# Three layer norms run tile by tile into the next product, and the last one stored in six parts

## What is computed

```
m = ada_modulation(c, w_ada, b_ada)
h = x * (1.0 + m[:, 1]) + m[:, 0]
x = post_norm_residual(x, swiglu(h, w_ffn1_in, w_ffn1_out), m[:, 2], 0.5, ln_g[0], ln_b[0])
h = x * (1.0 + m[:, 4]) + m[:, 3]
...
x = post_norm_residual(x, mix, m[:, 5], 1.0, ln_g[1], ln_b[1])
h = x * (1.0 + m[:, 7]) + m[:, 6]
x = post_norm_residual(x, swiglu(h, w_ffn2_in, w_ffn2_out), m[:, 8], 0.5, ln_g[2], ln_b[2])
```

## Time and profile before

| | |
|---|---|
| Median of 3 runs | 1078.45 us (1078.01 to 1084.59) |
| The profiled execution | 1081.01 us |
| Its span, first to last instruction | 1079.2 us |
| Mean granted clock of TensorE | 0.915 of full speed |
| TensorE matmul busy | 913.4 us, 85% of the span |
| VectorE, ScalarE, GpSimd busy | 543.2, 353.2, 36.5 us |

### The profile page before, as it was taken

One profiled execution on the slowest core, in us unless ns is written; L12 is line 12 of the kernel. 1 busy time (PEld: TensorE's weight loads), 2 busy tenths in 40 slices (PEclk: granted clock), 3 DMA queues, 4 the chain that ended last, 5 costly groups with the idle time before them and its releaser, 6 DMA issues. The chain is left out here.

```text
span 1079.2 us, 17658 instructions
## 1 busy us (share of the span) xinstructions
PE 913.4 (85%) x7201; PEld 814.6 (75%) x7201; DVE 543.2 (50%) x813; ACT 353.2 (33%) x505; POOL 36.5 (3%) x42
## 2 busy tenths in 40 slices
PE   3679999999998699988775599777739999999983
PEld 2369999998996699845654577556729999989982
DVE  0144444445655633386557544371664555555653
ACT  2122232223342333346425133340232332233322
POOL 0000000000000000010000000000500000000000
PEclk9679999999999799989899889876969999999996
DMA  9958889885556542747595783969402555434501
GB/s 271 310 158 235 242 246 257 244 236 136 160 169 209 185 145 76 237 163 231 158 384 167 270 278 103 372 217 290 134 22 79 156 154 144 130 99 134 160 1 49
DMA packets 232790, 199.95 MB, mean 185 GB/s; under 512 B 9489, under 2 KB 198045, under 8 KB 232582
## 3 DMA queue, kind: packets, MB, share of 16 engines
q1 hardware_dynamic: 229376, 190.87, 58.1%
q10 hardware_dynamic: 2278, 4.16, 1.3%
q0 software_dynamic: 1056, 3.80, 1.0%
HBM read 195.00 MB, written 3.80 MB: 184 GB/s over the span
## 5 line engine op out<-in xcount | busy, mean ns | idle before, releaser
L575 PE MATMUL B<-Hh,wh 128*128 128x320 f32 x960 | 291.1, 316 | 28.2 <-DVE Hl L1443 17.4
L576 PE MATMUL B<-Hl,wh 128*128 128x320 f32 x960 | 288.2, 313 | 0.0
L1406 DVE TENSOR_TENSOR wl<-raw,wh 128x2048 fp32r<-128x2048 f32 x90 | 208.1, 2313 | 147.2 <-ACT wh L1063 147.2
L1063 ACT ACTIVATE wh<-raw 128x2048 fp32r<-128x2048 f32 x90 | 172.3, 1914 | 161.9 <-PE B L580 111.6
L575 PEld LDWEIGHTS B<-Hh,wh 128*128 128x128 f32 x960 | 184.2, 192 | 38.4 <-issue 38.4
L576 PEld LDWEIGHTS B<-Hl,wh 128*128 128x128 f32 x960 | 184.3, 192 | 0.0
L580 PE MATMUL B<-Hh,wl 128*128 128x320 f32 x960 | 161.2, 310 | 0.0
L580 PEld LDWEIGHTS B<-Hh,wl 128*128 128x128 f32 x960 | 146.8, 189 | 0.0
L575 PE MATMUL B<-Gh,wh 128*128 128x320 f32 x352 | 104.0, 309 | 4.6 <-DVE Gl L1503 4.6
L576 PE MATMUL B<-Gl,wh 128*128 128x320 f32 x352 | 103.7, 309 | 0.0
L737 PE MATMUL B<-cst,ring 128*128 128x128 f32 x512 | 72.1, 301 | 30.0 <-DMA ring<-in_cache_k 11.8
(11 more groups left out here) (211 smaller groups left out, 835.8 us busy)
## 6 DMA issues: line engine op xcount, KB each, us to landing
raw<-in_w_ffn_in SPq DMA_DIRECT2D x88, 512.0 KB, 6.4
raw<-in_w_ada SPq DMA_DIRECT2D x72, 512.0 KB, 4.7
ring<-in_cache_k SPq DMA_DIRECT2D x128, 256.0 KB, 4.4
ring<-in_cache_v SPq DMA_DIRECT2D x128, 256.0 KB, 4.6
raw<-in_w_ffn_out SPq DMA_DIRECT2D x32, 384.0 KB, 3.6
raw<-in_w_mix_in SPq DMA_DIRECT2D x24, 512.0 KB, 4.8
raw<-in_w_ffn_out SPq DMA_DIRECT2D x32, 320.0 KB, 4.3
raw<-in_w_mix_out SPq DMA_DIRECT2D x4, 512.0 KB, 8.6
```

Source lines behind the costliest of these rows:

```text
L575: pe.matmul(out, w, xh[k], start=start and k == 0, stop=False)
L576: pe.matmul(out, w, xl[k], start=False, stop=False)
L1063: return act.activation(out, in_, func, **kw)
L1406: dve.tensor_tensor(wl[:, wbuf(n), :], raw_view(n), f32(wh[:, wbuf(n), :]), ALU.subtract).then_inc(lo_ready, 1)
```

## The change

- **Fused weights.** For the second and third sublayer `fuse_affine` folds g and b of the norm into the modulation's scale and shift, once, on vectors of 72 columns. The input of the next product is then made from `Z` directly, as `Z * rstd * scale + shift`, into a new buffer `scaled`; ScalarE adds the prompt's shift while it rounds.
- **Tile by tile.** `modulate` makes the samples first, then prompt tiles one at a time, two ahead of the `Hl` that VectorE makes between them. ScalarE rounds one tile at a time. `first_slot` replaces the first `pair_slot` of F1, MI and F2: its first bank takes tile k as soon as `Hh` and `Hl` of tile k are there, then comes the second bank, then the low weights of both.
- **Stream made later.** `X` of the first and second norm is made by `stream`, one tile behind each of eight `low` in MI, and behind each of eight slots of F2.
- **Mean and variance.** GpSimd adds six tiles; the last two go into the mean through matmuls of their own. Eps is the bias of ScalarE's root, which reads PSUM; L1477 goes.
- **Order.** In A2 two modulation slots come ahead of the mean and a third ahead of the variance, and ScalarE copies two rows before it squares. At the start `modulate(0)` comes ahead of `low(F1 + 1)`. In the second norm `low(F2 + 1)` moves behind the subtractions. ScalarE rounds the input of MI before it rounds the weights of MI + 1.
- **Output.** VectorE scales `X` per tile, ScalarE adds b, TensorE transposes in the order half, token tile; six PSUM banks are used, VectorE copies four groups and ScalarE two, and SyncE stores six parts. GpSimd's two stores and its last wait go.

```diff
+                fs = slice(512 * half, 512 * half + 512)
+                dst = o["y_prompt"][t0:t0 + tn, fs] if t < 2 else o["y_sample"][:, fs]
+                sp.dma_start(dst, xn[0:tn, t, fs]).then_inc(y_stored, 16)
...
+            def first_slot(t, kind, b0, s):
...
+                wait_high(t)
+                for h in range(2):
+                    for k in range(KT):
+                        if h == 0:
+                            pe.wait_ge(hh_ready, 9 * s + k + 2)
+                            pe.wait_ge(hl_ready, 9 * s + k + 2)
+                        pe.matmul(B[b0 + h][:, 0:N], part(vh, h, k), Hh[:, k, :], start=(k == 0), stop=False)
+                        pe.matmul(B[b0 + h][:, 0:N], part(vh, h, k), Hl[:, k, :], start=False, stop=False)
+                wait_low(t)
+                for h in range(2):
+                    for k in range(KT):
+                        m = pe.matmul(B[b0 + h][:, 0:N], part(vl, h, k), Hh[:, k, :], start=False, stop=(k == KT - 1))
+                m.then_inc(used, 1)
...
             def norm_mean(s):
                 pe.wait_ge(zsum_ready, s + 1)
-                pe.matmul(B[2][:, 0:N], C("mean"), zsum[:, :], start=True, stop=True).then_inc(mean_ready, 1)
+                pe.matmul(MEAN, C("mean"), zsum[:, :], start=True, stop=False)
+                pe.wait_ge(z_ready, KT * s + KT - 1)
+                pe.matmul(MEAN, C("mean"), Z[:, KT - 2, :], start=False, stop=False)
+                pe.wait_ge(z_ready, KT * s + KT)
+                pe.matmul(MEAN, C("mean"), Z[:, KT - 1, :], start=False, stop=True).then_inc(mean_ready, 1)
...
-                    pair_slot(At(F1 + 2 * j + 1, i, 4), "ffn_in", 2 * j)
+                    if i == 0 and j == 0:
+                        first_slot(At(F1 + 1), "ffn_in", 0, 0)
+                    else:
+                        pair_slot(At(F1 + 2 * j + 1, i, 4), "ffn_in", 2 * j)
...
+            first_slot(At(MI), "wide", 0, 1)
...
+            first_slot(At(F2), "ffn_in", 0, 2)
+            pair_slot(At(F2 + 1), "ffn_in", 2)
...
+            for n, (half, t) in enumerate(Y_GROUPS):
+                t0, tn = TILES[t]
+                for k in range(4 * half, 4 * half + 4):
+                    if t == 0:
+                        pe.wait_ge(x_final, k + 1)
+                    m = pe.transpose(Y_BANKS[n][0:tn, (k % 4) * P:(k % 4 + 1) * P], X[:, k, t0:t0 + tn], ident)
+                m.then_inc(y_T, 1)
...
             def round_input(s):
 
-                for j in range(4):
-                    act.wait_ge(h_ready, 4 * s + j + 1)
-                    act_(Hh[:, 2 * j:2 * j + 2, :], Z[:, 2 * j:2 * j + 2, :]).then_inc(hh_ready, 1)
+                src = scaled if s else Z
+                act.wait_ge(hs_ready, s + 1)
+                act_(Hh[:, :, S:N], src[:, :, S:N]).then_inc(hh_ready, 1)
+                for k in range(KT):
+                    act.wait_ge(h_ready, KT * s + k + 1)
+                    if s:
+                        act_(Hh[:, k, 0:S], src[:, k, 0:S], ACT.Identity, bias=mod[:, 3 * s * KT + k, 0:1]
+                             ).then_inc(hh_ready, 1)
+                    else:
+                        act_(Hh[:, k, 0:S], src[:, k, 0:S]).then_inc(hh_ready, 1)
...
             def norm_root(s):
-                act.wait_ge(veps_ready, s + 1)
-                act_(rstd[:, :], rstd[:, :], ACT.Sqrt).then_inc(std_ready, 1)
+                act.wait_ge(sq_used, 4 * s + 4)
+                act_(rstd[:, :], VAR, ACT.Sqrt, bias=C("eps")).then_inc(std_ready, 1)
...
-            norm_squares(0)
             for k in range(6):
                 if k == 2:
+                    norm_squares(0)
                     norm_root(0)
                 act.wait_ge(used, A2 + k + 1)
                 act.wait_ge(ada_comb, 29 + k)
                 act_(arow[:, k % 2, :], B[4 + k % 2][:, 0:256]).then_inc(ada_row, 1)
             high(At(MI))
+            round_input(1)
             high(At(MI + 1))
-            round_input(1)
...
+            for k in range(KT):
+                act.wait_ge(x_scaled, k + 1)
+                b = PRM_AT["ln_b"] + 2 * KT + k
+                act_(X[:, k, :], X[:, k, :], ACT.Identity, bias=prmT[:, b:b + 1]).then_inc(x_final, 1)
+            for n in Y_ON_ACT:
...
+            def fuse_affine(s):
+
+                sc, sh = mod[:, (3 * s + 1) * KT:(3 * s + 2) * KT, :], mod[:, 3 * s * KT:(3 * s + 1) * KT, :]
+                lo = (s - 1) * KT
+                g, b = [prmT[:, PRM_AT[name] + lo:PRM_AT[name] + lo + KT].unsqueeze(2).broadcast_to([P, KT, NC])
+                        for name in ("ln_g", "ln_b")]
+                step(dve.tensor_tensor(affine[:, :, :], sc, b, ALU.mult))
+                step(dve.tensor_tensor(sh, sh, affine[:, :, :], ALU.add))
+                step(dve.tensor_tensor(sc, sc, g, ALU.mult))
...
+                ds = dst[:, :, S:N].rearrange("p k (b t) -> p k b t", b=NB)
+                src = (Z if s else X)[:, :, S:N]
+                if s:
+                    r = rstd[:, S:N].unsqueeze(1).broadcast_to([P, KT, NS])
+                    step(dve.tensor_tensor(dst[:, :, S:N], src, r, ALU.mult))
+                    src = dst[:, :, S:N]
+                step(dve.tensor_tensor(ds, src.rearrange("p k (b t) -> p k b t", b=NB), samples(3 * s + 1), ALU.mult))
+                dve.tensor_tensor(ds, ds, samples(3 * s), ALU.add).then_inc(hs_ready, 1)
+
+                def prompt(k):
+                    sc = mod[:, (3 * s + 1) * KT + k, 0:1]
+                    if s:
+                        m = dve.scalar_tensor_tensor(out=dst[:, k, 0:S], in0=Z[:, k, 0:S], scalar=sc, in1=rstd[:, 0:S],
+                                                     op0=ALU.mult, op1=ALU.mult)
+                    else:
+                        m = dve.tensor_scalar(dst[:, k, 0:S], X[:, k, 0:S], sc, mod[:, k, 0:1], ALU.mult, ALU.add)
                     m.then_inc(h_ready, 1)
-                for j in range(4):
-                    dve.wait_ge(hh_ready, 4 * s + j + 1)
-                    dve.tensor_tensor(Hl[:, 2 * j:2 * j + 2, :], Z[:, 2 * j:2 * j + 2, :],
-                                      f32(Hh[:, 2 * j:2 * j + 2, :]), ALU.subtract).then_inc(hl_ready, 1)
+
+                def rest(k):
+                    dve.wait_ge(hh_ready, 9 * s + k + 2)
+                    hh = f32(Hh[:, k, 0:S])
+                    if s:
+                        m = dve.scalar_tensor_tensor(out=Hl[:, k, 0:S], in0=dst[:, k, 0:S],
+                                                     scalar=mod[:, 3 * s * KT + k, 0:1], in1=hh, op0=ALU.add,
+                                                     op1=ALU.subtract)
+                    else:
+                        m = dve.tensor_tensor(Hl[:, k, 0:S], dst[:, k, 0:S], hh, ALU.subtract)
+                    m.then_inc(hl_ready, 1)
+
+                prompt(0)
+                prompt(1)
+                dve.wait_ge(hs_ready, s + 1)
+                dve.wait_ge(hh_ready, 9 * s + 1)
+                dve.tensor_tensor(Hl[:, :, S:N], dst[:, :, S:N], f32(Hh[:, :, S:N]), ALU.subtract).then_inc(hl_ready, 1)
+                for k in range(KT):
+                    dve.wait_ge(h_ready, KT * s + k + 1)
+                    rest(k)
+                    if k + 2 < KT:
+                        prompt(k + 2)
...
+            def stream(s, k):
+
+                g, b = PRM_AT["ln_g"] + s * KT + k, PRM_AT["ln_b"] + s * KT + k
+                step(dve.scalar_tensor_tensor(out=X[:, k, :], in0=Z[:, k, :], scalar=prmT[:, g:g + 1], in1=rstd[:, :],
+                                              op0=ALU.mult, op1=ALU.mult))
+                step(dve.tensor_scalar(X[:, k, :], X[:, k, :], prmT[:, b:b + 1], None, ALU.add))
...
-                between(0)
-                dve.wait_ge(sq_used, 4 * s + 4)
-                dve.tensor_scalar(rstd[:, :], B[3][:, 0:N], LN_EPS, None, ALU.add).then_inc(veps_ready, 1)
...
+                between()
+                dve.wait_ge(d_ready, 4 * s + 4)
                 dve.wait_ge(std_ready, s + 1)
                 step(dve.reciprocal(rstd[:, :], rstd[:, :]))
-                for j in range(4):
-                    zj = Z[:, 2 * j:2 * j + 2, :]
-                    step(dve.tensor_tensor(zj, zj, two(rstd[:, :]), ALU.mult))
-                    for k in (2 * j, 2 * j + 1):
-                        g, b = PRM_AT["ln_g"] + s * KT + k, PRM_AT["ln_b"] + s * KT + k
-                        m = dve.tensor_scalar(X[:, k, :], Z[:, k, :], prmT[:, g:g + 1], prmT[:, b:b + 1],
-                                              ALU.mult, ALU.add)
-                    if s == 2 and j == 3:
...
             scale_vec(1)
             dve.wait_ge(x_copied, KT)
+            modulate(0)
             low(At(F1 + 1))
-            modulate(0)
             low(At(F1 + 3))
...
+            fuse_affine(1)
...
+            fuse_affine(2)
+
+            for k in range(8):
+                low(At(MI + k + 2))
+                stream(0, k)
...
+                if k < 3:
+                    low(At(MO + k + 2))
```

(11 more changed lines are left out.)

105 lines of the change are left out of this document (43 added, 62 removed).

## The result

| | before | changed |
|---|---|---|
| median of four runs each (us) | 1080.01 | 1046.41 |
| lowest to highest | 1078.01 to 1084.59 | 1037.77 to 1049.8 |
| ratio, 95% interval | | 0.967 [0.960, 0.974] |
| profiled execution, span (us) | 1081.01, 1079.2 | 1045.4, 1043.4 |
| mean granted clock | 0.915 | 0.923 |

The forecast was 1048.2, range 1038 to 1057. In a second comparison, five rounds on another chip, the changed kernel took 1042.26 and the one before 1081.97: 0.964 [0.959, 0.968]. An execution more than 1.5% above the fastest of its kernel counts as slow and is left out of the ratios; the only one here is the profiled one of `wait_all` (1058.22 us).

The account below looks back on a forecast made before the run. TensorE, busy 85% of the span, was taken to bound the kernel, with loss left at four stage edges: start and three norms. Gains 5.4 + 6.0 + 11.1 + 7.8 = 30.3 us off 1078.45 gave 1048.2 us, range 1038 to 1057.

Parts of the forecast that it names:

- The start, 5.4: Start to the end of F1's first slot: slot ends at 65.6 in place of 71.05, 5.4 us gained.
- the tile's 0.83 us: F1's first slot: VectorE makes one tile and the rest of another in 0.41 + 0.42 = 0.83 us.
- rival (1): First slots: the clock is already up when the second bank starts, 5.9 us less, 1042.3; chance 0.17.
- rival (4): F1 starts earlier than its weights can come, so the start's 5.4 us are lost, 1053.6; chance 0.05.
- The first norm, 6.0: First norm to the end of MI's first slot: it ends at 364.0 in place of 370.0, 6.0 us gained.
- The second norm, 11.1: Second norm to the end of F2's first slot: it ends at 806.5 in place of 817.7, 11.1 us gained.
- The last norm and output, 7.8: Third norm to the end: last copy at 1066.5 in place of 1073.58, and a faster store, 7.8 us gained.
- one add less and no L1477: Third norm: these two savings bring the reciprocal 1.6 us forward, to 1059.2.
- 0.7 for the store: After the last copy: a 256 KB part lands in 4.6 us where 5.6 stood, counted as 0.7 us gained.
- What I cost at nothing: Added `fuse_affine` and `stream` work on VectorE: covered by idle time; uncovered, all sixteen `stream` steps would cost 15 us.
- (2): First slots: the ScalarE-VectorE hand-over sets the pace, 1.2 us a tile, 8.6 us more, 1056.8; chance 0.10.
- (3): The clock doesn't come back in the first slots, 1054.2, chance 0.09; with many slots low, chance 0.02.

Follow-up runs that it names:

- wait_all: The changed kernel, but the first slots of F1, MI and F2 wait for all nine input parts: 1046.42 us, 0.968; repeated, 1052.18 us, 0.974.
- one_mean: The changed kernel, but GpSimd adds all eight tiles and the mean is one matmul: 1046.09 us, 0.970.
- two_stores: The changed kernel, but SyncE stores the result in two parts after all six copies: 1047.41 us, 0.973.
- stream_first: The changed kernel, but the normed stream is made between reciprocal and modulation again, as before the change: 1060.04 us, 0.982.

## Why the prediction was right, point by point

**The four edges** are where the gain is, most of it at the second norm and the output as foreseen, and all work between them has kept its length to 0.02 us but for O1's start and the attention. The time, 1046.4 for 1048.2, is closer than its terms, and that is luck: the edges gave 40.75 us, not 30.3, and 4.9 at O1 and in the attention part, which the forecast had at nothing, went the other way.

**The start, 5.4, was 7.97.** Of its steps the tile's 0.83 us failed: I added recorded durations, 0.41 and 0.42, where the distance between two starts is 0.33. That and an earlier first tile make 1.0. The slot then ended 5.8 us after its last tile where I had 7.15, since the clock rose 1.7 us after that tile and not 4.6: rival (1) in part. F1's weights came in time, so rival (4) is out.

**The first norm, 6.0, was 7.84.** The reciprocal came 12.8 us behind O1's last residual in place of the 13.9 of my sum: the variance began 0.8 us earlier than before, where I had it begin as before, and took 4.63 us in place of 5.00. From the reciprocal on I had 18.35, and it was 17.6: the clock rose 3.6 us after the last tile.

**The second norm, 11.1, was 13.15.** Half of the missing 2.05 is the variance, 6.34 us where it took 7.48 before, the other half the slot (6.0 us from its last tile). The first half isn't shown to be the change's: in other profiles the variance takes 6.23 us in the kernel before and 7.41 in the changed one. This edge is 42.2 us in the mean of two profiles of before and 30.5 in the mean of five with the changed code, a gain of 11.6. The terms for GpSimd's adds, L1477 and the stream held.

**The last norm and output, 7.8, was 11.79.** From the reciprocal to the last copy 7.24 for 7.3. But 1.6 for the norm was 3.8: the step "one add less and no L1477" left out that the variance behind it would run at the full clock, which `one_mean` showed (2.0 us come back as variance). And 0.7 for the store was 2.5: the row of 4.6 us for loads of 256 KB was the wrong measure. Parts of 256 KB landed in 2.3 us here, and the last part, which has 128 KB and not 256, in 2.5. By the Trainium skill, page "DMA: Bandwidth & Descriptors", section "Anatomy of one DMA — SWDGE (gpsimd) path", the estimate is 2.6 us for 256 KB and 2.3 for 128; the trace sides with the page, although its figures are for GpSimd's path and these stores go by SyncE's queue. `two_stores` showed that the parts do it, not SyncE's queue.

**What I cost at nothing.** `stream` is covered, even twice over. `fuse_affine` stands in `stream_first` too, where O1 takes its old 12.41 us. What I didn't see at all is the 1.5 us at O1: in ten of the eleven profiles without fillers there the clock falls behind the 2.1 us wait for `Gl`; in `stream_first` and twice in the kernel before, with the same wait, it doesn't. Filling the wait takes it away in the one profile that there is. At the start of O2, behind a wait of 2.46 us, the same fall comes in one of two profiles of the kernel before and in four of eleven of changed kernels without fillers there. So such a fall comes and goes without the change; whether the change makes it likelier at O1, two profiles of before can't tell, and what decides is open.

**The attention part's 3.4 us** is of the size of its spread (two profiles of before, 301.2 and 305.7, are within that of the others). Whether the change costs something there, the mean being 3 us higher, can't be settled with two profiles of before. The second comparison of times, 39.7 us, agrees with the edges' 40.75 less O1's 1.5; the first, 33.6, is 6 us lower, and the attention part alone varies by more than that.

**The rivals.** (1) held in part at the first slots, 3.0 of its 5.9 us; at the third variance, where it had no price, the clock gave 2.3 more. (2), 1.2 us a tile, is wrong: 0.66 and 0.79. ScalarE and VectorE overlap and VectorE sets the pace. (3): the low clock doesn't outlast a first slot. The Trainium skill, page "TensorE: Matmul & The Clock Gate", section "HAM oscillation — how this bites in real kernels", has the full clock lost to the waits between bursts of matmuls. The traces agree in kind, in F2's tiles after the fillers and in O1, at 0.8 to 1.5 us a place and not as slots on end.

## What to carry to other kernels

At the edge between two stages of a saturated engine, first move everything off the path that the next product doesn't need; here that was worth some 15 us, the tile-wise start of the product 10, the new output 5. Take the pace of a chain from the distance between starts in the timeline, since recorded durations overlap. And when a wait ahead of a short burst of TensorE goes, count what the clock gives back in that burst, and what an idle stretch of 2 us elsewhere may take: a few matmuls into an unused bank between the mean and the variance brought the reciprocal 1.7 us forward, of which the next slot gave back 0.9. Fillers ahead of a product cost time too when the clock is low: five of them held up a first slot whose input was there.

## What the runs showed of the hardware that I had not expected

- Back to back on VectorE, 128x256 instructions recorded at 0.41 to 0.42 us start every 0.33 us, three-operand ones of 0.48 every 0.395.
- The same eight matmuls of the variance take 4.65 us or 6.1 to 7.5 in the second and third norm. Without fillers all stand behind a wait of 1.68 us: in the third norm they are fast with the split mean in ten profiles of eleven, in the second norm slow with either mean, and fast there with three fillers in the wait, twice.
- A product fed tile by tile brought the clock up in F1 before the unbroken work was 2 us old, yet lost it in F2 with fillers ahead of it, and kept it in MI.
- Identical code in the attention part takes 299.8 to 312.5 us from one execution to the next, with the granted clock of a 20 us window at 0.70 or 0.91.
- A store of 1 MB lands 4.2 us after its issue, one of 256 KB issued 0.44 us behind it after 4.7, and parts of 256 KB issued one by one after 2.3.
